# The sum over the experts moved into the second block's program: bias and one row of four on TensorE, residual and first norm tile by tile, overflow blocks with rows of their own in memory

## What is computed

```python
# first block, per layer (one layer)
x = x + gt1 * rms_norm(mix, g_post_mix[l])                    # MLA and sparse attention before this
h2 = rms_norm(x, g_pre_ffn[l]) * (1.0 + sc2) + sh2
ffn = moe_ffn(h2, ...)                                        # 32 experts, 4 of them per token
x = x + gt2 * rms_norm(ffn, g_post_ffn[l])
# inside moe_ffn: tokens are sorted by expert and run in blocks of 128
hid = xb @ w_mlp1[e] + b_mlp1[e]
act = glu * jax.nn.sigmoid(SWIGLU_ALPHA * glu) * (lin + 1.0)
y   = act @ w_mlp2[e] + b_mlp2[e]
out = segment_sum(y * slot_gate, slot_tok)                    # four gated rows per token
# second block, per layer (two layers)
h = rms_norm_2(x, attn_norm_w[layer]); proj = h @ w_in[layer]
```

## Time and profile before

| | us |
|---|---|
| median of three runs | 3333.4 |
| the profiled execution, its own time | 3338.27 |
| span of the profiled execution, first to last instruction | 3336.5 |
| TensorE busy in it | 2934.3 (88%) |
| last matmul of the experts ends | 1835.2 |
| first dense matmul of the second block starts | 1939.3 |

### The profile page before, as it was taken

The page is one execution under the profiler, slowest core; times in us unless marked ns, Lnnn a source line. Parts: engine busy times, 40 slices in busy tenths (PEclk is TensorE's granted clock), DMA queues, the critical chain, the costliest instruction groups (busy, mean ns, idle before and its releaser), DMA issues. The chain is left out here.

```text
span 3336.5 us, 41343 instructions
## 1 busy us (share of the span) xinstructions
PE 2934.3 (88%) x13577; PEld 2323.4 (70%) x13577; DVE 2202.6 (66%) x3091; ACT 1619.3 (49%) x2099; POOL 85.8 (3%) x98
## 2 busy tenths in 40 slices
PE   7766797379999999999999178889999998899998
PEld 5544565358888888888887066568888775578887
DVE  6546753469999999999998446555444455554444
ACT  5322232168888888888886042433322224432332
POOL 0000000100000000000000200000000000000000
PEclk9876658589999999999999589999999999999999
DMA  9300000279999999999996331123333321132332
GB/s 355 123 19 0 4 1 1 108 275 362 390 389 379 390 388 379 391 384 385 390 381 274 124 125 57 32 77 94 101 95 101 105 70 41 51 108 82 95 101 88
DMA packets 263765, 610.35 MB, mean 183 GB/s; under 512 B 21356, under 2 KB 113276, under 8 KB 263640
## 3 DMA queue, kind: packets, MB, share of 16 engines
q1 hardware_dynamic: 246176, 549.59, 45.0%
q0 software_dynamic: 10816, 37.11, 3.1%
q10 hardware_dynamic: 6648, 22.00, 1.6%
HBM read 583.38 MB, written 25.24 MB: 182 GB/s over the span
## 5 line engine op out<-in xcount | busy, mean ns | idle before, releaser
L1180 DVE TENSOR_TENSOR weights_low<-pieces,weights_high 128x1024 fp32r<-128x1024 f32 x768 | 891.3, 1219 | 73.6 <-ACT weights_high L1173 64.0
L1173 ACT ACTIVATE weights_high<-pieces 128x1024 fp32r<-128x1024 f32 x768 | 804.8, 1061 | 204.0 <-PE banks L373 203.1
L371 PE MATMUL banks<-weights_high,xT_high 128*128 128x512 f32 x1024 | 404.3, 395 | 1.3 <-DVE weights_low L1180 1.3
L372 PE MATMUL banks<-weights_low,xT_high 128*128 128x512 f32 x1024 | 400.4, 391 | 0.0
L373 PE MATMUL banks<-weights_high,xT_low 128*128 128x512 f32 x1024 | 400.1, 391 | 0.0
L1885 ACT ACTIVATE weights_high<-pieces 128x1024 fp32r<-128x1024 f32 x192 | 201.1, 1054 | 356.3 <-DMA pieces<-in_w_up 256.7
L1889 DVE TENSOR_TENSOR weights_low<-pieces,weights_high 128x1024 fp32r<-128x1024 f32 x192 | 233.7, 1223 | 127.7 <-ACT weights_high L1885 126.6
L371 PE MATMUL banks<-hT_high,weights_high 128*128 128x512 f32 x704 | 283.6, 403 | 2.8 <-DVE hT_low L2818 2.8
L372 PE MATMUL banks<-hT_low,weights_high 128*128 128x512 f32 x704 | 275.8, 392 | 0.0
L373 PE MATMUL banks<-hT_high,weights_low 128*128 128x512 f32 x704 | 275.3, 391 | 0.0
L371 PEld LDWEIGHTS banks<-weights_high,xT_high 128*128 128x128 f32 x1024 | 193.2, 189 | 52.7 <-issue 13.7
(11 more groups left out here) (408 smaller groups left out, 4693.4 us busy)
## 6 DMA issues: line engine op xcount, KB each, us to landing
pieces<-in_w_mlp SPq DMA_DIRECT2D x768, 512.0 KB, 7.7
pieces<-in_w_up SPq DMA_DIRECT2D x64, 512.0 KB, 4.1
pieces<-in_w_down SPq DMA_DIRECT2D x64, 512.0 KB, 3.3
pieces<-in_w_in SPq DMA_DIRECT2D x56, 512.0 KB, 5.2
pieces<-in_w_ada SPq DMA_DIRECT2D x48, 512.0 KB, 8.7
expert_out<-y ACTq DMA_DIRECT2D x32, 512.0 KB, 7.6
pieces<-in_w_out SPq DMA_DIRECT2D x16, 512.0 KB, 4.3
pieces<-in_w_o SPq DMA_DIRECT2D x8, 512.0 KB, 5.2
```

What stands on the lines that cost most here:

```text
L371: nc.tensor.matmul(out, a[0], b[0], start=start, stop=False)
L372: nc.tensor.matmul(out, a[0], b[1], start=False, stop=False)
L1173: self.core.nc.scalar.activation(self.hi[:, c % E_PARTS, :], self.raw[:, c % E_RAW, :], ACT.Copy).then_inc(self.high.sem, 1)
L1180: self.core.nc.vector.tensor_tensor(self.lo[:, c % E_PARTS, :], self.raw[:, c % E_RAW, :], self.hi[:, c % E_PARTS, :], ALU.subtract).then_ ...
```

## The change

1. `combine_stage`, `residual_stage` (behind the experts) and `clear_stage` are gone, and so are the clearing of `ffn` and the load of `iota` in `more_blocks_stage`. 65 semaphores are now cleared by POOL at the start of `experts_stage`; the second block's stream and the experts have semaphores of their own.
2. The overflow blocks, when they run, store their rows to `expert_out`, which grows from 128 to 512 rows per expert. The routing no longer masks gates and slots. POOL fills the 384 further rows of each expert with zeros: 32 DMAs of 1024 runs of 1536 bytes, 50.3 MB in all, issued inside the MLA `attention_stage` (`aside`), and waited for by POOL at the start of the routing's scatter.
3. The second block's first six pieces are loaded by SyncE at the end of `experts_stage`, into places of the experts' ring that have been split. The gain of the feed-forward norm goes through memory (`ffn_gain`).
4. `second_block` begins with the sum. POOL fetches six rows, then issues the nine constants, then the other ten rows, each when its place is free. TensorE turns the gates, forms the bias of a tile in a pair of banks, and adds row 0 to it as a product with a diagonal matrix of the gates (made on ScalarE). VectorE adds rows 1 to 3. Residual, norm, transposition follow tile by tile, interleaved.

```diff
@@ class Moe
+        self.slots = nc.dram_tensor("expert_out", [E * ROWS, D], F32).ap()
+    def zero_later_blocks(self, pool):
+        zeros = self.core.mask[:, 0:S - P]
+        rows = (BLOCKS - 1) * CAP * D // (P * (S - P))
+        for e in range(E):
+            later = self.slots[e * ROWS + CAP:(e + 1) * ROWS, :].rearrange("r d -> (r d)").rearrange("(p b n) -> p b n", p=P, n=S - P)
+            pool.dma_start(later, zeros.unsqueeze(1).broadcast_to([P, rows, S - P])).then_inc(self.zeroed.sem, 16)
@@ routing_stages, gpsimd
+            pool.wait_ge(*moe.zeroed(16 * E))
             pool.wait_ge(*slots_ready(1))
@@ experts_stage
+                for p in range(PLACES):
+                    sp.wait_ge(*moe.low(PER_EXPERT * E - E_RAW + p + 1))
+                    stream.load(sp, p)
...
+                for s in over:
+                    pool.sem_clear(s.sem)
@@ second_block, gpsimd
+                for i in range(TOP_E * T):
+                    if i == ROW_PLACES:
+                        for dst, src in loads:
+                            pool.dma_start(dst, src).then_inc(constants.sem, 16)
+                    if i >= ROW_PLACES:
+                        t, j = (i - ROW_PLACES) // TOP_E, (i - ROW_PLACES) % TOP_E
+                        pool.wait_ge(*(rows_multiplied(t + 1) if j < ROWS_PE else rows_added(ROWS_DVE * t + j - ROWS_PE + 1)))
+                    pool.indirect_dma_start(slot_rows[:, i % ROW_PLACES, :], None, moe.slots, ...)
@@ second_block, tensor
+                def multiply_rows(t):
+                    for j in range(ROWS_PE):
+                        i = TOP_E * t + j
+                        pe.wait_ge(*diag_ready(ROWS_PE * t + j + 1))
+                        pe.wait_ge(*fetched[i % ROW_PLACES](16 * (i // ROW_PLACES + 1)))
+                        for n in range(2):
+                            last = nc.tensor.matmul(psum[:, SUM_BANK[t] + n, :], diag[:, ROWS_PE * t + j, :], slot_rows[:, i % ROW_PLACES, n * BANK:(n + 1) * BANK], start=False, ...)
+                    last.then_inc(rows_multiplied.sem, 1)
...
+                        turn_gates()
+                        for t in range(3):
+                            bias_rows(t)
+                        for t in range(3):
+                            multiply_rows(t)
+                        bias_rows(3)
                         turn_h(0, 0)
-                        turn_h(0, 1)
+                        multiply_rows(3)
@@ second_block, scalar
+                act.dma_start(b2[0:E, :], W["b_mlp2"][0]).then_inc(ffn_loads.sem, 16)
+                act.dma_start(ffn_gain[:], moe.gain.partition_broadcast(P)).then_inc(ffn_loads.sem, 16)
...
+                square_ffn(0)
+                square_ffn(1)
+                root_ffn(0)
+                square(0, 0)
+                square_ffn(2)
+                root_x(0, 0)
...
@@ second_block, vector
+                add_rows(0)
+                add_rows(1)
+                mean_ffn(0)
+                add_ffn(0)
+                add_rows(2)
+                mean_x(0, 0)
+                mean_ffn(1)
+                normalise(0, 0)
+                add_ffn(1)
+                low_h(0, 0)
+                add_rows(3)
+                mean_x(0, 1)
+                mean_ffn(2)
+                normalise(0, 1)
+                add_ffn(2)
+                low_h(0, 1)
...
```

More of the change, by code:

```diff
@@ L545, in attention_stage, with _ @@
         with nc.Block() as block:
+            if aside is not None:
+                @block.gpsimd
+                def _(pool):
+                    aside(pool)
             @block.tensor
@@ L1318, in experts_stage @@
     last_first, last_second = W1_PIECES - 1, W2_PIECES - 1
+    mine = [index_ready, x_turned, xT_high, xT_low, lin_taken, glu_taken, sigmoid_ready, act_ready, act_turned, actT_high, actT_low, y_taken, expert_chosen, stored,
+            begun, b1_full, b1_open, b1_high, b1_low, moe.high, moe.low, moe.used] + gathered + moe.full
+    over = [s for n, s in core.events.items() if s.base and n not in POOL_SIGNALS and s not in mine]
     with ExitStack() as ctx:
@@ L1564, in more_blocks_stage @@
     rows = core.event("more_rows")
-    weights, index, turned, copied, hidden, acted, product, y_ready, sigmoid, gates_made, gates_turned, spread = signals
+    weights, index, turned, copied, hidden, acted, product, y_ready, sigmoid, stored = signals
     banks = core.psum
@@ L1570, in more_blocks_stage @@
         w1, idx = sb("more_w1", [P, KD, 2 * F]), sb("more_idx", [P, 1], I32)
-        w2, b1 = moe.raw[:, 0:W2_PIECES, :], moe.raw[:, W2_PIECES:W2_PIECES + 2, :].rearrange("p r n -> p (r n)")
-        iota, gates, gT = sb("more_iota", [P, S]), sb("more_gates", [P, T, P]), sb("more_gatesT", [P, T, P])
-        with nc.Block() as block:
-            @block.vector
-            def _(dve):
-                nc.vector.memset(more[:], 0.0)
-        load_stage(core, [(iota[:], W["iota"])], "more_loads")
+        free = E_RAW - PLACES
+        w2_first, w2_last, b1 = moe.raw[:, PLACES:E_RAW, :], sb("more_w2", [P, W2_PIECES - free, PIECE]), sb("more_b1", [P, 2 * F])
+        w2 = [w2_first[:, k, :] if k < free else w2_last[:, k - free, :] for k in range(W2_PIECES)]
         glu = hid[:].rearrange("p (n two) -> p two n", two=2)[:, 0, :]
@@ L1646, in _ @@
                             last.then_inc(y_ready.sem, 1)
[L1647 to L1648 removed]
+                            act.wait_ge(*y_ready(1))
+                            act.dma_start(moe.slots[bass.ds(e * ROWS + b * CAP, CAP), :], xg[:]).then_inc(stored.sem, 16)
+                            act.wait_ge(*stored(16))
                         @block.vector
@@ L1799, in close @@
         self.core.sb("region", [P, self.size // 4], ctx=ctx)
-def clear_stage(core, signals):
-    nc = core.nc
-    with nc.Block() as block:
-        @block.gpsimd
-        def _(pool):
-            for s in signals:
-                pool.sem_clear(s.sem)
-    for s in signals:
-        s.base = 0
 def level_mix(t, first, count, n):
@@ L2017, in _ @@
             def _(sp):
-                for p in range(L2 * LAYER_PIECES):
+                for p in range(PLACES, L2 * LAYER_PIECES):
                     stream.load(sp, p)
@@ L2361, in split, with square_ffn, root_ffn, root_x @@
                         stream.split_high(act, layer * LAYER_PIECES + p)
+                def square_ffn(t):
+                    act.wait_ge(*rows_added(ROWS_DVE * (t + 1)))
+                    if t:
+                        act.wait_ge(*ffn_squares(t))
+                    nc.scalar.activation(ffn_junk, ffn[t], ACT.Square, accum_out=ffn_ms[:, t:t + 1]).then_inc(ffn_squares.sem, 1)
+                def root_ffn(t):
+                    act.wait_ge(*ffn_spread(t + 1))
+                    nc.scalar.activation(ffn_root[:, t:t + 1], ffn_mean[:, t:t + 1], ACT.Sqrt).then_inc(ffn_rooted.sem, 1)
                 def square(layer, t):
-                    if layer:
-                        act.wait_ge(*added(layer - 1, 56 + 2 * t + 2))
+                    act.wait_ge(*(added(layer - 1, 56 + 2 * t + 2) if layer else x_new(t + 1)))
+                    if t and not layer:
+                        act.wait_ge(*squares(layer, t))
                     nc.scalar.activation(junk, x[:, t, :], ACT.Square, accum_out=ms[:, 0, t:t + 1]).then_inc(squares.sem, 1)
+                def root_x(layer, t):
                     act.wait_ge(*spread(layer, t + 1))
```

281 lines of the change are left out of this document (137 added, 144 removed).

## The result

The changed kernel takes 3372.7 us (median of 4 runs, 3368.97 to 3379.68) where the kernel before, on the same chip, takes 3332.6. The ratio is 1.0122, 95% interval 1.0109 to 1.0134: it is **slower by 1.2%**, 40 us. The profiled execution took 3370.64 us, with a span of 3368.8. The two profiled executions lie only 32 us apart, since that of the kernel before (3338.27) was slower than its median; all differences read from traces are set against that.

The account below looks back on a forecast made before the run. The prediction took a chain of small waits, neither an engine nor the memory, to bound the junction between the blocks. 40.5 us gained less 3 lost gave 37.5 off 3338.27, 3300.8, as a median 3296 us; 8-in-10 range 3284 to 3326.

Parts of the forecast that it names:

- The junction: Between the experts' last store and the second block's steady work: small waits taken out or overlapped, 40.5 us gained.
- slot 2: Second block, where TensorE's steady work begins: forecast at 1917.0 us instead of 1957.5, some 81 behind the last store.
- The rival of the clock: Junction: TensorE's clock rises during the sum, calls cost 0.88 us instead of 1.75, time 3288 us; chance 0.08.
- Two readings ahead of it: Junction in the old profile: the clock strip's hole read as two fives, and VectorE as mostly idle from 1836 to 1914.
- The price of the zeros: MLA attention: POOL's 32 fills hidden in its 98 us, only the key positions' load behind it delayed, 3 us lost.
- a queue that holds some ten transfers hides the drain: MLA attention: argument against the fills holding the stage, where waiting for earlier fills would be 4.0 us each.
- my middle value: MLA attention: POOL's issue of one fill taken as 1.94 us, a fetch beside busy VectorE, 62 us in all.
- My rival of the fills: MLA attention ends only when POOL has issued all 32; middle form 3313 us, chance 0.11; hard form 0.09.
- Its hard form: MLA attention: 4.6 us an issue of a fill, stage ends 48 us late, 3344 us; chance 0.09.
- The 3 us that I put on the key positions: Behind the MLA attention: their load shares the queue with fills, about 6 us instead of 3.0; loss between 0 and 8.
- everything after slot 2 hangs on what it hung on before: Second block behind the junction: reason given for measuring the change at slot 2; no cost put on what follows.
- my chain: Step-by-step estimate of the new junction, with the fills' cost: 37.5 us off, 3296 us, own range 3288 to 3304; chance 0.60.

Follow-up runs that it names:

- runs 6 and 7: Run 5 with 30 (or 31) zero fills in the MLA attention and the last 2 (or 1) in the sparse attention: 3334.25 and 3340.75 us.
- run 5: Changed kernel with its four kept small tiles (672 bytes) allocated ahead of the weights' region instead of behind it: 3347.51 us, 1.0033 of before.
- run 9: Run 5 with all 32 fills issued by SyncE instead of GpSimd and the key positions loaded by ScalarE: 3327.36 us, 0.9984 of before.
- run 4: Kernel before with 32 bytes put ahead of the weights' stream, so that weights and `hT` move together: 3333.36 us, 0.9996 of before.
- run 10: Kernel before with 128 bytes put between weights_high and the rest of the second block's tiles: 3357.41 us, 1.0051 to 1.0096 of before.
- run 3: Kernel before with 32 unused bytes put between weights_high and the rest of the second block's tiles: 3362.77 us, 1.0085 of before.
- run 8: Run 5 with 15 fills in the MLA attention, 15 in the sparse attention and 2 in the routing: 3294.06 us, 0.9868 of before.
- run 1: Changed kernel with the flag tile `more_blocks` made 64 bytes wide, moving the second block's tiles 32 bytes further: 3366.57 us, 1.0094 of before.

## Why the prediction was wrong

**The junction was right.** Forecast: slot 2 80.8 us behind the last store. Measured: 78.57, 42.7 gained instead of 40.5. The other traces with this junction have 78.3 to 78.7, and 81.9 and 81.7 in runs 6 and 7, which no run explains. Its links, counted from the last store: the first bias call 9.5 us behind it (11.2 forecast), the turning of tile 0 begun at 45.0 (46.9), the first dense matmul at 48.9 (52.4), the turning of tile 3 begun at 73.0 (74.8), slot 2 5.6 us behind that (6.0). The twelve instructions of the first six bias calls took 10.60 us (10.5). One price I had forgotten, TensorE's 8.89 us of "issue" at the start of the new block, after which it turned the gates, 7.8 us behind the store; it just fitted in ahead of the bias, for which I had expected to wait longer, until the gain was loaded. And the clock rose sooner than I gave it, 0.70 over the stretch from the last store to slot 2 where the earlier trace rows had 0.53, so the four calls of the row products of tiles 0 and 1 took 1.44 us each instead of 1.75 and the two of the last bias 1.11. The rival of the clock was partly true. Two readings ahead of it were loose, without harm to the sum: the strip of the clock has a 5 and an 8 in its hole, not two fives, and VectorE, at work for 39.3 of the 78 us in the earlier trace rows, was not mostly idle.

**The price of the zeros was the first failure**: 3 us forecast, 51 measured. The step that failed is "a queue that holds some ten transfers hides the drain". The issue itself was cheaper than my middle value, 0.87 us against 1.94. (The Trainium skill, "DMA: Bandwidth & Descriptors", on the anatomy of a DMA on the GpSimd path, has many descriptors emitted before the cost of each shows; the trace agrees, at 1024 runs, until the fifteenth fill.) The 1.94 was no price of a busy VectorE in the first place: the fetch right behind it in the earlier trace rows, 1.08 us, stands beside the same four multiply-adds (1858.70 to 1864.16). By issues alone the 28 us would have been hidden, and I weighed only the issues. The traffic, which I let end anywhere from 426 to 590 because the first wait for it stood at 638, was in truth waited for at once: the block's closing drain on GpSimd. 50.3 MB at 332 GB/s are 152 us in a stage of 98; that is the 51. My rival of the fills named the right wait among its reasons, "wait until earlier fills have drained", but at 4.0 us each, which by its own sum makes the stage 30 us late and not 51: the rate was 332 GB/s and not 392, 4.7 us a fill. Its hard form (48 us, 3344, chance 0.09) comes near run 5, which has nothing but this and took 3347.5, by luck: its 4.6 us were an issue that grows with the runs, and the issues took 0.87. The Trainium skill, "SBUF — State Buffer", on its two sides, which I had brought for the 1.94, played no part that can be seen: beside VectorE at work for 87 of 98 us the issues of the fills took 0.87.

The 3 us that I put on the key positions did not come: their load met no traffic, since all had drained. (In run 9 it did meet some, and took 3.8 us more.) The 2.6 us more between there and the store of `h_rows` are not the change's: run 9 apart, that distance is 192.1 to 195.7 us over the traces, and 195.2 in run 4, whose kernel differs from that before in nothing there. It goes with TensorE's granted clock, 0.65 on average over the stretch in the traces with 192.1 to 192.7 us and 0.63 to 0.64 in those with 194.5 and more. The 3.1 us less in the experts' stretch are of that kind too: 1242.4 to 1243.1 us at a clock of 0.96, run 10 among them, and 1245.3 to 1245.9 at 0.95.

**The second failure is a term left at zero.** The step is "everything after slot 2 hangs on what it hung on before": that is true of the waits, and I took it for the time. I had also written that I was wrong "if the stretches after slot 2 have another length than before", but gave this no chance and no price. They are 24.4 us longer. The diff puts four small tiles, 672 bytes in all, between the weights and the second block's other tiles, and I read that as a matter of space. Runs 3 and 4 show that it is a matter of rate; run 5 shows that nothing else in the change has part in it (1376.4 us from slot 2 to the end, against 1379.0; over the traces at the full rate this distance is 1370.7 to 1379.3).

The sum by what was measured: -42.7 + 51.1 + 2.6 - 3.1 + 24.4 = +32.3. Without the two failures, in run 8, it is 3294, which my chain gave as 3296, and 41 us below the kernel before of its set, where my chain had 37.5. That it comes so near is no credit to the prediction: a change is priced with its side effects.

What stays open: why a distance that is no multiple of 256 bytes slows a matmul (by 5 to 7 ns in the mean of the stretch), and which of the two reads is held. The remainders on dividing by 256 that were tried are 0, 32, 128, 160 and 192. The runs change the distance of all pairs at once. And that the memory paces SyncE's issues was argued from the rate in the trace; no run varies it. Why GpSimd stands after fifteen fills stays open likewise: one size of fill was tried.

## What to carry to other kernels

A transfer that "nobody waits for" still has an end that somebody meets: look for the instruction that closes the block on the queue that sent it, and divide the bytes by the measured rate before you call them hidden. Spread over stages that each outlast their share, the same 50 MB cost nothing.

When a change moves allocations, compare the step of unchanged, back-to-back matmuls before and after, as the first thing. Where TensorE is the bound, as in this second block, keep its operands a multiple of 256 bytes apart; small tiles go in front of the large ones, together or padded.

## What the runs showed of the hardware that I had not expected

- The step between the full-size matmuls of these products at full clock is 226 to 227 ns (443 in 100 us) when the distance in a partition between stationary and moving tile is a multiple of 256 bytes. At 32, 128, 672 or 704 bytes more, 429 to 434 fit in 100 us, and the median step is 228 to 237 ns, depending on the pair of tiles. The absolute address doesn't matter (runs 4 and 5). Over the second block this is worth 19 us (704 bytes, run 1 less run 5) to 29 us (32 bytes, run 3) in 3333.
- GpSimd takes 15 transfers of 1024 runs of 1536 bytes (368 packets each in the trace) at 0.87 us each, then stands 58 us; its drain at the end of a block lasted up to 64.5 us and ended 0.4 to 1.1 us after the last packet of its fills. SyncE's drain took 0.37 us with 3.4 MB under way, and its issues of the same fills (1024 packets each) took 4.02 us each.
- 332 GB/s of stores beside the attention left VectorE's work as it was: 87.3 us in a stretch of 98, against 86.9 without them.
